# Layer 0's experts: the second expert's gate and up loads stand ahead of the front's loads on SyncE

## The chip, the cores and the metric

The kernel runs on one core of a Trainium2 chip. A core has five engines that run their own instruction streams and meet at semaphores: TensorE (PE, matrix products), VectorE (DVE), ScalarE (ACT), GpSimd (POOL) and SyncE (SP), which here only issues DMA transfers. All transfers of a core share 16 DMA engines. The metric is the device time of one execution in microseconds (us).

## What is computed

Two layers of a transformer trunk over 1024 tokens and 256 context tokens, width 1024, all in float32: a mixer (attention, and in layer 1 a state space scan), then a mixture of 16 experts in which each expert chooses its tokens (128 tokens and 32 context tokens each). The change lies in layer 0's experts:

```python
def expert_choice_ffn(h, w_router, w_gate, w_up, w_down):
    b, n, _ = h.shape
    cap = CAPACITY_FACTOR * n // N_EXPERTS
    aff = jax.nn.softmax(jnp.einsum('bnd,de->bne', h, w_router).astype(jnp.float32), axis=-1)
    gate, idx = lax.top_k(jnp.swapaxes(aff, 1, 2), cap)
    bidx = jnp.arange(b)[:, None, None]
    xg = h[bidx, idx]
    hid = jax.nn.silu(jnp.einsum('becd,edf->becf', xg, w_gate)) * jnp.einsum('becd,edf->becf', xg, w_up)
    out = jnp.einsum('becf,efd->becd', hid, w_down) * gate[..., None].astype(h.dtype)
    return jnp.zeros_like(h).at[bidx, idx].add(out)
...
def trunk_layer(x, ctx, c, c_ctx, common, mixer, ctx_out):
...
    x = x + gt1 * rmsnorm(mix, g_post_mix)
    h = rmsnorm(x, g_pre_ffn) * (1 + sc2) + sh2
    x = x + gt2 * rmsnorm(expert_choice_ffn(h, w_router, w_gate, w_up, w_down), g_post_ffn)
```

Behind it comes layer 1's first part, `front`: the residual sum, its norm and the projections of layer 1.

## The kernel before

`experts` does layer 0's 16 experts one after another. An expert has three weights of 4 MB: gate, up and down, each loaded in two halves of 2 MB (128 partitions x 8 x 512 numbers). There is one buffer for each weight (`wg`, `wu`, `wd`), so a half can be loaded only when the expert before has read it.

On TensorE an expert is `hidden_rows` (eight steps f, each 16 products with gate and 16 with up; steps 0 to 3 read the first half, 4 to 7 the second; `gu_done` counts the steps), `turn_rows` of the next expert's tokens, `down_ctx` (64 products for the context tokens, which need `hid` and `wd`), and seven `multiply` groups that form the down product by a scheme with seven products of half blocks instead of eight. For these VectorE forms sums of blocks of `wd` (`weight_sum`). The first of them, `weight_sum(e, 5)` (L2625), stands in VectorE's stream between the seventh and the eighth `hidden` (L2615), and waits for both halves of `wd`.

SyncE's stream sets the order of the loads. It is written out by hand, and SyncE works it off in that order: a load that waits for a semaphore holds back all behind it. For the first experts it is: gate and up of expert 0, the storing of a third of layer 1's modulation (`store_third`), `wd` of expert 0, a second third, and then

- `following.load`, the loads of layer 1's front (`FrontAhead.load`, L2336 to L2353): 6 loads of 512 KB, 2 of 1 MB and 64 KB (`wk`), 11 of 4 KB that spread a vector over the partitions element by element (`shift`, `gain`, `g`, `cw`), 4 of 4 KB in rows (`alog`, `dtb`)
- `load_gates_up(1)`, gate and up of expert 1 (L2453, L2454), each half behind a wait for `gu_done`: the first half for four steps of expert 0, the second for all eight
- `following.load_columns`, two loads of 2 MB for the front (L2357)
- `load_down(1)`, `wd` of expert 1 (L2461), behind a wait for the last products and sums of expert 0
- a loop over the other experts, each with `load_gates_up` and `load_down`.

What `following` loads goes to buffers of its own and is first read when `front` begins, after the last expert.

Of the kernel before, what the change touches and what calls it, by code (L numbers as in the profile page):

```python
# [153 lines left out]
def columns(ap):  # L154

    return ap.rearrange("(k p) -> p k", p=P)
# [2218 lines left out]
def experts(nc, name, K, listed, normed, mod, g_pre, w_gate, w_up, w_down, moe, following, down, last_third):  # L2375
# [7 lines left out]
    with Stage(nc, name) as st:  # L2383
# [43 lines left out]
        def multiplied(e, p):  # L2427
            return START + e * 7 + (7 + PRODUCTS.index(p) + 1)
# [7 lines left out]
        def sums_at(e, p):  # L2436
            return START + e * 4 + (4 + (5, 7, 6, 4).index(p) + 1)
# [4 lines left out]
        def half_of(weights, e, h):  # L2442
            return weights[bass.ds(e, 1), :, h * BANK:(h + 1) * BANK].rearrange("a (k p) n -> p (a k) n", p=P)

        with nc.Block() as block:

            @block.sync
            def _(sp):
                def load_gates_up(e):

                    for h in range(2):
                        sp.wait_ge(gu_done, START + e * 8 + HALF * (h + 1))
                        sp.dma_start(wg[:, h], half_of(w_gate, e, h)).then_inc(w_in["wg"][h], 16)  # L2453
                        sp.dma_start(wu[:, h], half_of(w_up, e, h)).then_inc(w_in["wu"][h], 16)  # L2454

                def load_down(e):

                    sp.wait_ge(mm_done, multiplied(e - 1, 7))
                    sp.wait_ge(sums_done, sums_at(e - 1, 4))
                    for h in range(2):  # L2460
                        sp.dma_start(wd[:, h], half_of(w_down, e, h)).then_inc(w_in["wd"][h], 16)  # L2461

                for c in range(conds):
                    sp.dma_start(shift[:, c, :], columns(mod[c, 3 * D:4 * D])).then_inc(vec_in, 16)
                    sp.dma_start(gain[:, c, :], columns(mod[c, 4 * D:5 * D])).then_inc(vec_in, 16)
                sp.dma_start(g[:], columns(g_pre)).then_inc(vec_in, 16)
                for n in range(opening.slots, opening.steps):
                    opening.load(sp, n)
                load_gates_up(0)
                opening.store_third(sp, 0)  # L2470
                sp.wait_ge(tp_done, START + 1)
                sp.wait_ge(opening.multiplied, START + opening.steps)
                load_down(0)
                opening.store_third(sp, 1)
                following.load(sp)
                load_gates_up(1)
                following.load_columns(sp)
                load_down(1)
                with sp.Fori(1, E - 1) as e:
                    load_gates_up(e + 1)  # L2480
                    load_down(e + 1)
                for h in range(2):
                    sp.wait_ge(gu_done, START + E * KD + HALF * (h + 1))
                    for n in range(h * HALF, (h + 1) * HALF):
                        closing.load(sp, n)
                st.renew(sp)
                sp.wait_ge(s_done, E * PLACED)
# [1645 lines left out]
```

## Time and profile before

| | us |
|---|---|
| median of 3 runs (3326.73 to 3328.04) | 3327.41 |
| the profiled execution | 3320.73 |
| its span, first to last instruction | 3318.9 |
| TensorE busy in the span | 3094.6 (93%) |
| VectorE, ScalarE, GpSimd busy | 1729.6, 1031.1, 567.1 |

The layer 0 experts run from about 1068 us to 1918 us of the span. The views used below are the timeline of an engine (one line for a run of like instructions: start, duration, engine, source line, tile written and tiles read, and in brackets the idle time before it and what ended it) and the table of stretches, which gives for each stretch the busy time of the engines, TensorE's granted clock as a share of full speed, the mean busy share of the 16 DMA engines and what they moved. On SyncE's timeline a duration is the time until the load is issued; its data land later.

### The profile page before, as it was taken

The page shows a single profiled execution, that of the slowest core. Times are in us where ns is not written, and L with a number is a line of the kernel's source. Part 1 is how long each engine was busy: PE and PEld are TensorE (multiplying, and loading weights), DVE is VectorE, ACT ScalarE, POOL GpSimd, SP SyncE. Part 2 cuts the span into 40 slices and gives each one's busy share as a digit, 9 for nine tenths or more (in the row PEclk, how much of TensorE's full clock was granted, in tenths as well). Part 3 has the DMA queues.
Part 4 walks back from the last instruction along what each step waited for, and adds up shares of the span by engine and source line. Part 5 has one row for each costly group of instructions (what it writes and reads, how often), then busy time and mean ns, then how long its engine had stood idle before and what let it go on. Part 6 is the DMA issues. An engine that isn't in the chain of part 4 may idle for free. (4 is left out here: it accounts for less than half of the span.)

```text
span 3318.9 us, 55367 instructions
## 1 busy us (share of the span) xinstructions
PE 3094.6 (93%) x20487; PEld 2210.7 (67%) x20487; DVE 1729.6 (52%) x3294; ACT 1031.1 (31%) x2319; POOL 567.1 (17%) x685
## 2 busy tenths in 40 slices
PE   6999989989996999999999979999899399999998
PEld 4888855667542888889898855566664255555554
DVE  3312068868646233232333353467785766666666
ACT  4111156756340111111111152245554222222222
POOL 0010224310110111111112130065101101111113
PEclk9999999999996999999999989999899699999999
DMA  6335454043538987778778750122314589999998
GB/s 237 133 111 105 83 190 143 17 110 113 198 146 311 307 308 262 264 261 282 254 262 271 270 192 2 67 72 88 101 34 173 204 303 336 335 333 333 330 330 334
DMA packets 345473, 680.82 MB, mean 205 GB/s; under 512 B 84904, under 2 KB 134056, under 8 KB 339104
## 3 DMA queue, kind: packets, MB, share of 16 engines
q1 hardware_dynamic: 310848, 576.46, 50.2%
q0 software_dynamic: 15920, 47.32, 5.6%
q10 hardware_dynamic: 18560, 55.19, 4.5%
q8 instruction: 81, 1.33, 0.2%
q14 instruction: 64, 0.52, 0.1%
HBM read 594.04 MB, written 91.03 MB: 206 GB/s over the span
## 5 line engine op out<-in xcount | busy, mean ns | idle before, releaser
L2751 PE MATMUL experts_gu_ps<-experts_xT,experts_wg 128*128 128x160 f32 x2048 | 303.2, 301 | 7.7 <-DVEq L2610 5.1
L2751 PE MATMUL experts_gu_ps<-experts_xT,experts_wu 128*128 128x160 f32 x2048 | 299.8, 299 | 0.0
L2751 PEld LDWEIGHTS experts_gu_ps<-experts_xT,experts_wg 128*128 128x128 f32 x2048 | 287.0, 191 | 13.6 <-issue 8.4
L2615 DVE TENSOR_TENSOR experts_hid<-experts_sil,experts_gu_ps 128x160 f32<-128x160 f32 x128 | 41.1, 321 | 489.2 <-ACT experts_sil L2561 489.2
L2751 PEld LDWEIGHTS experts_gu_ps<-experts_xT,experts_wu 128*128 128x128 f32 x2048 | 286.0, 190 | 0.0
L2561 ACT ACTIVATE experts_sil<-experts_gu_ps 128x160 f32<-128x160 f32 x128 | 38.9, 304 | 533.9 <-PE experts_gu_ps L2751 533.9
L3496 PE MATMUL front_pb_ps<-kept_hT,front_ahead_w 128*128 128x512 f32 (+1 forms) x384 | 139.0, 521 | 0.7 <-DVE kept_dt L3562 0.7
L3184 PE MATMUL experts_w_ps<-experts_wd,experts_hT 128*128 128x512 f32 x256 | 130.8, 597 | 8.5 <-issue 7.8
L3184 PE MATMUL experts_v_ps<-experts_wd,experts_hT 128*128 128x512 f32 x256 | 129.6, 592 | 0.0
L563 PE MATMUL proj_x_ps<-first_w,first_shared 128*128 128x256 f32 x480 | 114.7, 382 | 3.1 <-DMA first_w<-in_l_w_in 3.1
L4018 PE MATMUL scan_f_ps<-scan_w,kept_hT 128*128 128x512 f32 x256 | 116.3, 597 | 0.0
L3496 PEld LDWEIGHTS front_pb_ps<-kept_hT,front_ahead_w 128*128 128x128 f32 x384 | 72.3, 190 | 62.7 <-issue 59.4
L2516 POOL DMA_INDIRECT moe<-experts_yc,experts_ixsc x16 | 39.8, 2490 | 432.9 <-ACT experts_yc L2575 432.9
L644 DVE TENSOR_TENSOR proj_ob<-proj_z_ps,proj_kept 128x256 f32<-128x256 f32 x30 | 12.7, 424 | 191.0 <-PE proj_z_ps L563 190.1
L2953 ACT ACTIVATE experts_kept<-experts_x_ps 128x256 f32<-128x256 f32 x96 | 36.9, 384 | 234.6 <-PE experts_x_ps L3176 234.6
L563 PEld LDWEIGHTS proj_x_ps<-first_w,first_shared 128*128 128x128 f32 x480 | 91.5, 191 | 15.8 <-DMA first_w<-in_l_w_in 3.4
L876 ACT ACTIVATE attn_a_e<-attn_a_e,attn_a_nmx 128x1280 f32<-128x1280 f32 (+1 forms) x80 | 96.6, 1209 | 7.5 <-DVE attn_a_e L938 7.5
L2917 POOL DMA_INDIRECT moe<-experts_y,experts_ixs x15 | 24.1, 1609 | 414.3 <-DVE experts_y L3094 414.3
L3184 PEld LDWEIGHTS experts_w_ps<-experts_wd,experts_hT 128*128 128x128 f32 x256 | 47.3, 190 | 65.5 <-issue 64.5
L3184 PEld LDWEIGHTS experts_v_ps<-experts_wd,experts_hT 128*128 128x128 f32 x256 | 48.6, 190 | 61.2 <-issue 61.2
L1038 PE MATMUL attn_a_o_ps<-attn_a_v,attn_a_aT 128*128 128x128 f32 x672 | 83.5, 278 | 3.9 <-ACT attn_a_sq L891 3.9
L938 DVE TENSOR_SCALAR_CACHE_REDUCE attn_a_e<-attn_a_s_ps,attn_a_nmx 128x256 f32<-128x256 f32 (+1 forms) x128 | 72.7, 612 | 27.4 <-PE attn_a_s_ps L1013 27.4
(601 smaller groups left out, 6618.2 us busy)
## 6 DMA issues: line engine op xcount, KB each, us to landing
experts_wg<-in_l_w_gate SPq DMA_DIRECT2D x64, 2048.0 KB, 8.0
experts_wu<-in_l_w_up SPq DMA_DIRECT2D x64, 2048.0 KB, 12.8
down_ahead_wd<-in_l_w_down SPq DMA_DIRECT2D x32, 2048.0 KB, 15.8
experts_wd<-in_l_w_down SPq DMA_DIRECT2D x32, 2048.0 KB, 9.5
down_ahead_wd<-in_l_w_mod SPq DMA_DIRECT2D x16, 1024.0 KB, 9.0
proj<-proj_ob ACTq DMA_DIRECT2D x60, 256.0 KB, 2.3
first_w<-in_l_w_in SPq DMA_DIRECT2D x6, 2048.0 KB, 10.0
attn_a_mod_w<-in_l_w_mod ACTq DMA_DIRECT2D x12, 1024.0 KB, 7.3
```

Of the source, the lines that this page charges most:

```text
L563: mm = nc.tensor.matmul(to[:, left], by[k], at[k], start=(k == 0 and n in (0, 1, 5)), stop=(k == HALF - 1 and n in (3, 5, 6)), skip_group_ ...
L876: nc.scalar.activation(e[:, s, m, 0:w], e[:, s, m, 0:w], ACT.Exp, bias=nmx[:, s, m:m + 1], scale=-1.0, accum_out=sums[:, s, m:m + 1]).then ...
L938: nc.vector.tensor_scalar(e[:, s, m, c:c + w], S[i % 2][m][:, 0:w], -1.0, nmx[:, s, m:m + 1] if j else None, ALU.mult, ALU.min, accum_out= ...
L1038: mm = nc.tensor.matmul(O[:, 0:P], aT[:, kt, :], v[:, h % 2, kt, :], start=(kt * P == keys(t)[0]), stop=(kt == last))
L2516: pool.indirect_dma_start(moe.rearrange("t (j c) -> (t j) c", j=4), bass.IndirectOffsetOnAxis(ap=ixsc[:, 0:1], axis=0), yc[:], None, compu ...
L2561: nc.scalar.activation(sil[:, f % 2, :], GU[f % 2][:, 0, 0:N], ACT.Silu).then_inc(sil_done, 1)
L2615: nc.vector.tensor_tensor(hid[:, f, :], sil[:, f % 2, :], GU[f % 2][:, 1, 0:N], ALU.mult).then_inc(hid_done, 1)
L2751: mm = nc.tensor.matmul(GU[f % 2][:, part, 0:N], w[:, h, k, c * P:(c + 1) * P], xT[:, k, :], start=(k == 0), stop=(k == KD - 1))
L2953: nc.scalar.activation(kept[:, KEPT.index(p), :], bank[:, 0:COLS], ACT.Copy).then_inc(act_out, 1)
L3184: return nc.tensor.matmul(Y[h][:], hT[:, k, :], w[DOWN][:, k, h * BANK:(h + 1) * BANK], start=(k == 0), stop=(k == KD - 1))
L3496: mm = nc.tensor.matmul(pb[n % 4][:, 0:width], w[:, s, k, at:at + P], hT[:, k, first:first + width], start=(k == 0), stop=(k == KD - 1))
L4018: mm = nc.tensor.matmul(F[f % 2][:], kept.hT[:, k, t * P:(t + 1) * P], w[:, int(kind == "q"), k, :], start=(k == 0), stop=(k == KD - 1))
```

## The change

In SyncE's stream the call for expert 1's gate and up loads moves up by one call, over the front's loads. The waits inside the call move with it.

```diff
@@ -2472,8 +2472,8 @@
                 sp.wait_ge(opening.multiplied, START + opening.steps)
                 load_down(0)
                 opening.store_third(sp, 1)
+                load_gates_up(1)
                 following.load(sp)
-                load_gates_up(1)
                 following.load_columns(sp)
                 load_down(1)
                 with sp.Fori(1, E - 1) as e:
```

No other engine's stream differs. On SyncE, where the front's loads begin (`signal103` is `gu_done`; `signal81` and `signal82` count the sums and the stores of the modulation):

```order
 L2461 DMA down_ahead_wd<-in_l_w_down 128x8x512
 L266 DMA mod<-experts_shared 2x512 [waits signal81] x4
-L2338 DMA front_ahead_gate<-mod 128x1024 [waits signal82]
-L2338 DMA front_ahead_gate<-mod 128x1024
+L2453 DMA experts_wg<-in_l_w_gate 128x8x512 [waits signal103,signal82]
+L2454 DMA experts_wu<-in_l_w_up 128x8x512
+L2453 DMA experts_wg<-in_l_w_gate 128x8x512 [waits signal103]
+L2454 DMA experts_wu<-in_l_w_up 128x8x512
+L2338 DMA front_ahead_gate<-mod 128x1024 x2
 L2339 DMA front_ahead_gpost<-in_l_g_post_ffn 128x1024
 L2341 DMA front_ahead_xt<-res 128x1024 x3
```

The four gate and up loads now follow the modulation's store, and the front's first load stands behind the second wait for `gu_done`.

On SyncE, where the front's small loads end and expert 1's down weights follow (`signal106` and `signal109` are the counts that `load_down` waits for):

```order
 L2352 DMA front_ahead_cw<-in_l_conv_w 128x8x1 x5
 L2353 DMA front_ahead_cw<-in_l_conv_b 128x8x1
-L2453 DMA experts_wg<-in_l_w_gate 128x8x512 [waits signal103]
-L2454 DMA experts_wu<-in_l_w_up 128x8x512
-L2453 DMA experts_wg<-in_l_w_gate 128x8x512 [waits signal103]
-L2454 DMA experts_wu<-in_l_w_up 128x8x512
 L2357 DMA front_ahead_w<-in_l_w_in 128x8x512 x2
 L2461 DMA down_ahead_wd<-in_l_w_down 128x8x512 [waits signal109,signal106]
```

The front's small loads now run straight into its column loads and the down weights, which have the same loads ahead of them as before, in another order.

## Rows read from the trace of the kernel before

**Rows 1.** The page: its span, and TensorE's busy time, share and instructions.

```profile
span 3318.9 us, 55367 instructions
PE 3094.6 (93%) x20487; PEld 2210.7 (67%) x20487; DVE 1729.6 (52%) x3294; ACT 1031.1 (31%) x2319; POOL 567.1 (17%) x685
```

**Rows 2.** Timeline of TensorE, experts 0 to 3: start us, us, what, [idle before].

```profile
1068.02 3.91 PE L2751 MATMUL experts_gu_ps<-experts_xT,experts_wg 128*128 128x160 f32 x16 [5.13 <-DVEq L2610]
...
1084.81 2.34 PE L2751 MATMUL experts_gu_ps<-experts_xT,experts_wu 128*128 128x160 f32 x16
...
1102.20 2.34 PE L2751 MATMUL experts_gu_ps<-experts_xT,experts_wu 128*128 128x160 f32 x16
...
1119.95 1.90 PE L2714 MATMUL experts_y_ps<-experts_shared,experts_hid 128*64 128x256 f32 x16
1124.38 3.42 PE L2751 MATMUL experts_gu_ps<-experts_xT,experts_wg 128*128 128x160 f32 x16 [2.54 <-DMA experts_wu<-in_l_w_up]
1127.59 3.07 PE L2751 MATMUL experts_gu_ps<-experts_xT,experts_wu 128*128 128x160 f32 x16
...
1163.86 3.66 PE L2725 MATMUL experts_yc_ps<-down_ahead_wd,experts_hid 128*32 128x256 f32 x64 [1.28 <-DVE experts_hid L2615]
...
1179.69 2.44 PE L2751 MATMUL experts_gu_ps<-experts_xT,experts_wg 128*128 128x160 f32 x16
...
1195.00 2.34 PE L2751 MATMUL experts_gu_ps<-experts_xT,experts_wu 128*128 128x160 f32 x16
...
1231.97 2.44 PE L2751 MATMUL experts_gu_ps<-experts_xT,experts_wg 128*128 128x160 f32 x16
```

**Rows 3.** Timeline of VectorE around the second expert's first weight sum.

```profile
1157.20 0.32 DVE L2615 TENSOR_TENSOR experts_hid<-experts_sil,experts_gu_ps 128x160 f32<-128x160 f32 x1 [4.03 <-ACT experts_sil L2561]
1161.28 2.29 DVE L2625 TENSOR_TENSOR experts_shared<-down_ahead_wd 128x2048 f32<-128x2048 f32 x1 [3.76 <-DMA down_ahead_wd<-in_l_w_down]
1163.49 0.31 DVE L2615 TENSOR_TENSOR experts_hid<-experts_sil,experts_gu_ps 128x160 f32<-128x160 f32 x1
```

**Rows 4.** Timeline of SyncE's queue: start of issue us, us until issued.

```profile
1085.13 0.82 SPq L2338 DMA_DIRECT2D front_ahead_gate<-mod  x2
...
1108.32 0.58 SPq L2453 DMA_DIRECT2D experts_wg<-in_l_w_gate  x1
...
1120.65 13.07 SPq L2357 DMA_DIRECT2D front_ahead_w<-in_l_w_in  x2
1133.83 12.46 SPq L2461 DMA_DIRECT2D down_ahead_wd<-in_l_w_down  x2
...
1197.52 0.38 SPq L2453 DMA_DIRECT2D experts_wg<-in_l_w_gate  x1
...
1214.89 0.37 SPq L2453 DMA_DIRECT2D experts_wg<-in_l_w_gate  x1
```

**Rows 5.** Stretches: us, engines' busy us, granted clock, DMA share, GB/s.

```profile
1197.60:1850.00 652.40, 652.40 (x5611) 576.40 (x5611) 214.66 (x330) 94.98 (x227) 109.42 (x157) 1.00 0.78 266
...
1085.00:1086.00 1.00, 1.00 (x9) 1.00 (x9) 0.00 (x0) 0.00 (x0) 0.00 (x0) 1.00 0.06 25
...
1085.00:1110.20 25.20, 25.20 (x230) 23.20 (x231) 7.91 (x17) 3.49 (x10) 0.00 (x0) 1.00 0.83 177
1110.20:1161.20 51.00, 48.46 (x367) 44.30 (x364) 10.42 (x14) 5.33 (x13) 8.99 (x13) 0.97 1.05 372
...
1209.00:1211.00 2.00, 2.00 (x17) 2.00 (x16) 0.17 (x1) 0.30 (x1) 0.00 (x0) 1.00 0.60 220
1211.00:1213.00 2.00, 2.00 (x17) 2.00 (x16) 1.96 (x2) 0.00 (x0) 0.00 (x0) 1.00 0.00 0
1213.00:1215.00 2.00, 2.00 (x17) 2.00 (x16) 0.48 (x1) 0.16 (x1) 0.00 (x0) 1.00 0.00 0
1215.00:1216.00 1.00, 1.00 (x14) 0.83 (x12) 0.79 (x3) 0.15 (x1) 0.00 (x0) 1.00 0.11 6
1216.00:1217.00 1.00, 1.00 (x20) 0.65 (x22) 0.97 (x3) 0.75 (x3) 0.00 (x0) 1.00 0.87 137
```

## The prediction

> **What bounds the kernel now.** I began with the page. TensorE is busy for 93% of the span of 3318.9 us [rows 1], so the kernel is ahead wherever TensorE does not wait, and what a change of loads can move is the few places where it does. The stretches of time tell where these are: from 1197.6 us, in the third expert's gate products, to 1850 us TensorE is busy for 652.40 of 652.40 us [rows 5]. From there one expert takes 52.28 us (1179.69 to 1231.97, [rows 2]), and whatever shift the third expert starts with goes through to the end. So only the first two experts matter, and the timeline of TensorE shows two waits there [rows 2]:
>
> First, after the first expert's down products (last start 1119.95, 1.90 us) TensorE stands still until 1124.38, 2.54 us, released by the up weights `wu` of the second expert. After the stop its first two groups of 16 take 3.42 and 3.07 us, where the third expert's first takes 2.44 and the others 2.34: 1.71 us more. This is what the change goes for: 2.5 + 1.7, some 4.3 us.
>
> Second, at 1163.86 it starts the second expert's context products 1.28 us late, released by VectorE's last product for `hid`. The timeline of VectorE tells why that was late [rows 3]: VectorE is in order, and ahead of the last `hidden` stands `weight_sum(e, 5)` (L2625), which reads the down weights `wd`. It waited 3.76 us for them and began at 1161.28. So the landing of `wd` of the second expert sets the time at which TensorE goes on at 1163.86, and **TensorE arrives there early already**. Had the first wait not been there, the second would be 1.28 + 4.3 = 5.6 us long, and the third expert would begin when it does now. The question is then not how early the gate and up weights come but when `wd` lands.
>
> When it lands is a matter of the queue. The timeline of SyncE [rows 4] has the front's loads from 1085.13, the second expert's gate and up loads from 1108.32, the front's two column loads from 1120.65, `wd` from 1133.83. The stretches [rows 5] show the 16 DMA engines at a share of 0.83 from 1085 to 1110.2 and at 1.05 from 1110.2 to 1161.2: packed without a hole until `wd` is there. That landing moves by what is added to the queue ahead of it, bytes or holes.
>
> **The change, part by part.** No instruction and no byte is added or taken away; on SyncE four loads of 2 MB stand ahead of 23 loads of the front instead of behind them, and all 27 still stand ahead of `wd`. What changes is when the queue has something to do.
>
> (a) The first half of gate and up waits for TensorE to have read that half (`gu_done`). The front's first load now starts at 1085.13; the fourth pair of groups of the first expert ends at 1084.81 + 2.34 = 1087.15 [rows 2]. With the 0.15 us that such a load needs after its release (1197.34 to 1197.52 in the third expert, [rows 4]), the queue gets its first work at 1087.3, 2.2 us later than now.
>
> (b) The second half waits for all eight, 1102.20 + 2.34 = 1104.54 [rows 2], so it is issued at 1104.7. Behind this wait the front's 23 loads are queued, and nobody else feeds the queue. Before the change this wait cost nothing, because the loads stood so late that both halves were free. How long the queue stands empty is shown by a later expert, where the same two halves are issued 17.37 us apart (1197.52 and 1214.89, [rows 4]); here it is 17.4. There the share is 0.60 in 1209 to 1211, 0.00 until 1215, 0.11 in 1215 to 1216, 0.87 in the next us [rows 5]. Data end near 1210.2 and begin again near 1215.9: **a hole of 5.7 us**. In a later expert there is slack for it; here there is none.
>
> (c) The second expert's gate and up weights are then there by about 1100 and 1118 (issue plus 12.7 us as in the third expert: 1197.52 to 1210.2), TensorE wants them at 1121.8 and 17 us later. The first wait goes.
>
> (d) The front's loads are wanted after the last expert, beyond 1850 us; late by tens of us they cost nothing.
>
> (e) `wd` lands 2.2 + 5.7 = 7.9 us later, since what is ahead of it is the same. VectorE begins L2625 at 1161.28 + 7.9 = 1169.2 instead of 1161.28, and TensorE its context products at 1171.8 instead of 1163.86. It is free for them at 1162.58 - 4.3 = 1158.3, so it waits 13.5 us. Bounds of the 7.9: below, the front's stretch may pack better when a backlog stands before it. Its share of 0.83 over 25.2 us leaves 4.3 us unused, 0.9 of them at its start (0.06 in the first us, [rows 5]); so up to 3.4 us could come back, and 4.5 us be left. I take none of it: the stretch now has rows first and then many small loads of 4-byte elements, which SyncE must issue one after another in either order. Above, the first half moves its 4.19 MB in 12.7 less some 0.9 to begin, 11.8 us, where the 372 GB/s of the packed stretch make 11.3: 0.5 us more, and as much again for what GpSimd's transfers may do.
>
> (f) TensorE's clock. After the stop of 2.54 us the granted share fell and 1.71 us were lost; at 1068.02, after a stop of 5.13 us, the first group took 3.91 instead of 2.44, 1.5 us lost [rows 2]. Now a stop of 13.5 us stands ahead of the context products. Between 1.5 and 3.4 us (twice the 1.7); I take 1.9, near to the two rows, a little above since the stop is longer than either. The old loss of 1.7 no longer counts on the path, as it lay ahead of a wait that it only shortened.
>
> (g) After that: the third expert's first gate and up half stands right behind `wd`, 4.19 MB, 11.3 us by the same rate, there at some 1181; TensorE wants it at 1179.69 + 9.8 = 1189.5. Second half and next `wd` have more room. Nothing late comes after.
>
> **Sum:** 7.9 + 1.9 = 9.8 us slower. The profiled execution took 3320.73 us, 6.7 less than the median of the runs (3327.41), with a span of 3318.9; by it the new one would be 3330.5, its span 3328.7. I put the same difference on the median: 3337.2 us.
>
> **A rule that speaks for a smaller number.** Of the 25.2 us up to 1110.2 the queue's engines leave 17% unused [rows 5]. The Trainium skill, DMA: Bandwidth & Descriptors, section Bandwidth, gives 0.68 us for a 4 KB transfer (issued from GpSimd, where these come from SyncE). By it the front's 11 small column loads would be 7.5 us of the queue, and at the trace's rate the 4.2 MB of rows and key columns 11.3: 18.8 us for a stretch that now takes some 24. If a backlog hid all the rest, `wd` would land 2.5 us late and the sum be 4.4 us, an estimate from that page; it is the far end of R1 below. The trace's share leaves less room than that, and no row shows these loads behind a backlog.
>
> **Rivals.**
> *R1, the front's stretch packs.* As bounded in (e): `wd` lands 4.5 us late, the clock costs 1.5 to 1.9, the sum is 6.0 to 6.4, 3333.6 us. For it: 0.83 is not 1.05. Against: in the stretch SyncE issues without end from 1085.13 to 1108.32, 23.2 us, so that issuing is itself near the limit. It lies just inside 0.2% (6.7 us, 3334.1 us), which is about what a measurement of this kernel can tell from no change.
> *R2, faster: the gate and up wait was the real one.* If `wd` lands so early that VectorE finds it when it asks (1157.52 - 4.3 = 1153.2), TensorE gains 2.5 + 1.7 + 1.3 = 5.6 us: 3321.8 us. This needs `wd` to land 8 us earlier than now, by later loads overtaking the front's. For it only that the loads differ in kind; against it that the first wait ended with `wu`, which was behind the front's loads, and the share of 1.05. Every `wd` between costs or gains its own shift, and at an unmoved landing the change is worth 0 (3327.4).
> *R3, worse than forecast.* The clock takes 3.4 and the hole is longer by the gathers' traffic and the slower first half, 2 to 4 us: some 3341 to 3343. It decides from the point at which the third expert's weights land behind TensorE, 8 us later than in (g).
>
> **Chances.** Forecast (7.9 with its clock cost, 3334.5 to 3340) 0.66; R1 0.14; R2 0.07; an unmoved landing 0.04; R3 0.09. Faster by over 0.2%: half of R2 and little else reach 3320.8, and R2 stands 0.17% away, so 0.04. Slower by over 0.2%: the forecast, R3 and a third of R1, 0.79. Within: 0.17. The range leaves out R2 and the unmoved landing and the far end of R3: 3332.8 to 3341.
>
> **What would show it.** In the changed kernel: the first gate load of the second expert at 1087.3 and the third at 1104.7 on SyncE, a share of nearly 0 in between from 1100 to 1105.7; no wait of TensorE at 1121.8 and none for `wu`; the front's loads issued from 1106 to about 1140; VectorE's wait for `wd` at L2625 of some 16 us where 3.76 stand; TensorE's wait ahead of the context products of 13.5 us, and a granted clock below 1 behind it; the third expert's first gate product at 1189.5; everything later as before. I am wrong if `wd` lands before 1165, which would be the front's loads packing, or if TensorE does not wait there at all.

## The result, and the profile after

The change makes the kernel slower: a median of 3334.43 us over 15 runs against 3325.4 us over 15 runs of the kernel before, ratio 1.0022 with a 95% interval of 1.0016 to 1.0029. On 3325.4 us that is 7.3 us, 5.3 to 9.6; the plain difference of the two medians is 9.0 us, that of the two means 8.1. The forecast was 9.8 us: the direction and the mechanism held, the size was too large, and its sum lies just outside the interval. Of the 2.8 us between the forecast time, 3337.2, and the median, 2.0 are the start of the sum, 3327.41 from three runs, where fifteen give 3325.4. The two profiled executions (3330.26 and 3320.73 us) are single numbers in a spread of 6.5 us over runs of one kernel, so the traces are read below from a mark inside them.

TensorE of the changed kernel, with the columns of [rows 2]:

```profile
1069.36 4.55 PE L2751 MATMUL experts_gu_ps<-experts_xT,experts_wg 128*128 128x160 f32 x16 [5.14 <-DVEq L2610]
...
1075.92 2.34 PE L2751 MATMUL experts_gu_ps<-experts_xT,experts_wg 128*128 128x160 f32 x16
...
1123.74 2.44 PE L2751 MATMUL experts_gu_ps<-experts_xT,experts_wg 128*128 128x160 f32 x16
...
1171.94 5.68 PE L2725 MATMUL experts_yc_ps<-down_ahead_wd,experts_hid 128*32 128x256 f32 x64 [11.67 <-DVE experts_hid L2615]
...
1189.79 2.44 PE L2751 MATMUL experts_gu_ps<-experts_xT,experts_wg 128*128 128x160 f32 x16
...
1242.07 2.44 PE L2751 MATMUL experts_gu_ps<-experts_xT,experts_wg 128*128 128x160 f32 x16
```

The span is 3328.5 us. The wait for the up weights ahead of expert 1 is gone. In its place TensorE stands 11.67 us ahead of the context products, and these then take 5.68 us instead of 3.66. Expert 0 already began 1.3 us later in this execution and its first group took 0.6 more, which has nothing to do with the change, whose first moved load is issued only at 1089.23. So I count from expert 0's second step (1073.94 in the trace of before, 1075.92 here) to the first gate group of the fourth expert (1231.97 and 1242.07): 158.03 us before, 166.15 after, 8.1 more. Below this stretch is called **the interval**.

VectorE and SyncE of the changed kernel, which answer to [rows 3, 4]:

```profile
1169.36 2.29 DVE L2625 TENSOR_TENSOR experts_shared<-down_ahead_wd 128x2048 f32<-128x2048 f32 x1 [14.15 <-DMA down_ahead_wd<-in_l_w_down]
```

```profile
1089.23 0.39 SPq L2453 DMA_DIRECT2D experts_wg<-in_l_w_gate  x1
...
1106.54 0.37 SPq L2453 DMA_DIRECT2D experts_wg<-in_l_w_gate  x1
...
1107.87 3.99 SPq L2338 DMA_DIRECT2D front_ahead_gate<-mod  x2
...
1145.94 8.44 SPq L2461 DMA_DIRECT2D down_ahead_wd<-in_l_w_down  x2
```

VectorE waits 14.15 us for `wd` where it waited 3.76. SyncE issues the two halves of gate and up 17.3 us apart (1089.23 and 1106.54), and between them nothing. The stretches of the changed kernel show what the 16 DMA engines did meanwhile (columns as in [rows 5]; the share is the last but one):

```profile
1101.00:1103.00 2.00, 2.00 (x17) 2.00 (x16) 0.33 (x2) 0.30 (x1) 0.00 (x0) 1.00 0.39 143
1103.00:1105.00 2.00, 2.00 (x17) 2.00 (x17) 2.00 (x1) 0.00 (x0) 0.00 (x0) 1.00 0.00 0
1105.00:1107.00 2.00, 2.00 (x19) 2.00 (x17) 0.32 (x2) 0.30 (x1) 0.00 (x0) 1.00 0.00 0
1107.00:1109.00 2.00, 2.00 (x32) 1.39 (x34) 1.93 (x6) 0.98 (x3) 0.00 (x0) 1.00 0.65 124
```

By the shares, data end near 1101.8 and begin again near 1107.7, a hole of 5.9 us (5.7 were forecast).

### The profile page after: what moved, and what is told of

Same layout as the page of the kernel before. It is cut to its first block and busy times, and to the rows that moved or that the text cites. A ratio compares the mean times of both kernels' runs of the same rounds, so it can differ in the third digit from the quotient of the medians.

```text
span 3328.5 us, 55368 instructions
## 1 busy us (share of the span) xinstructions
PE 3095.2 (93%) x20487; PEld 2211.0 (66%) x20487; DVE 1728.7 (52%) x3294; ACT 1030.8 (31%) x2319; POOL 566.7 (17%) x685
```

## The experiments

My theory: the landing of expert 1's `wd` sets when the third expert begins; what comes ahead of it in the queue, bytes or holes, decides, and the wait for the up weights is worth nothing by itself. The main rival is that the early weights or their order against the front's loads cost by themselves. All edits are to the few lines in SyncE's stream, unless the text says otherwise. A ratio is the time against that of the kernel before, with its 95% interval. "Landing" below is the landing of `wd`'s second half, issue plus time to landing, counted from expert 0's second step.

### A second look at both kernels

Nothing is edited here.

> The kernel before once more, for a second trace. Question: how far the times of expert 1 vary from run to run when nothing is changed. In the experiment with wd ahead of the column loads TensorE's wait for the up weights was 1.1 us instead of 2.5 and the front's first load stood 1.7 us earlier against expert 0's steps. If that is only the run, these waits are again between 1 and 3 us here and the wait of VectorE for wd between 2 and 4.

> The changed kernel once more, for a second trace. Theory: its first gate load hangs on expert 0's fourth step and not on the modulation's store, so its times counted from expert 0's steps repeat within some 0.3 us: L2625 at 93.4 us after the second step, context products 5.2 to 5.7 us.

The kernel before, second trace:

```profile
1076.92 2.34 PE L2751 MATMUL experts_gu_ps<-experts_xT,experts_wg 128*128 128x160 f32 x16
...
1126.65 2.44 PE L2751 MATMUL experts_gu_ps<-experts_xT,experts_wg 128*128 128x160 f32 x16 [1.83 <-DMA experts_wu<-in_l_w_up]
...
1166.21 5.35 PE L2725 MATMUL experts_yc_ps<-down_ahead_wd,experts_hid 128*32 128x256 f32 x64 [3.04 <-DVE experts_hid L2615]
...
1236.01 2.44 PE L2751 MATMUL experts_gu_ps<-experts_xT,experts_wg 128*128 128x160 f32 x16
```

This trace alone shows that the first wait was covered. It is 1.83 us instead of 2.54 and the groups behind it lose nothing to the clock, so TensorE is 2.4 us earlier at the second wait; and there it waits 3.04 us instead of 1.28. VectorE's wait for `wd` was 5.52 us, beyond the 2 to 4 written down, and `wd` landed at 86.4 against 87.0. The clock's loss of 1.7 us now stands behind the second wait (5.35 against 3.66), where it counts: the interval is 159.09, against 158.03. The kernel before thus varies by itself, and its mean of two is 158.6 us.

The changed kernel repeated: L2625 at 93.2 us after the second step (93.4), the wait 11.45 (11.67), context products 5.66 (5.68), the interval 165.92 (166.15). Mean against mean the change costs 7.5 us (6.8 and 8.1 by single pairs), in agreement with the runs. `wd` lands at 86.7 before and 93.1 after: 6.4 us later.

### Only the first half ahead of the front's loads

Against the changed kernel:

```diff
-                load_gates_up(1)
+                load_gates_up(1, [0])
                 following.load(sp)
+                load_gates_up(1, [1])
                 following.load_columns(sp)
                 load_down(1)
```

(`load_gates_up` got a list of halves as an argument.)

> The changed kernel, but only the first half of expert 1's gate and up stands ahead of the front's loads; the second half, with its wait for all eight steps, stands behind them. Ahead of wd are the same loads, the queue starts as late as in the change (2.1 us), but has no hole. Theory (wd's landing sets the end, and holes in the queue move it): VectorE begins L2625 2.1 us later than in the kernel before, counted from expert 0's steps, TensorE waits 7 to 8 us ahead of the context products, the clock takes 1.5 to 2: 3.6 to 4 us slower than before. Rival A (the front's loads take longer once weights stand ahead of them, the hole is beside the point): as the change, 8 us slower. Rival B (the lost time is the early weights themselves, any such order costs the same): 8 us too.

```profile
1077.73 2.34 PE L2752 MATMUL experts_gu_ps<-experts_xT,experts_wg 128*128 128x160 f32 x16
...
1125.56 2.44 PE L2752 MATMUL experts_gu_ps<-experts_xT,experts_wg 128*128 128x160 f32 x16
...
1167.82 5.31 PE L2726 MATMUL experts_yc_ps<-down_ahead_wd,experts_hid 128*32 128x256 f32 x64 [5.73 <-DVE experts_hid L2616]
...
1237.58 2.44 PE L2752 MATMUL experts_gu_ps<-experts_xT,experts_wg 128*128 128x160 f32 x16
```

Ratio 1.0009 (1.0000 to 1.0018), interval 159.85 us. Rivals A and B, who had this as slow as the change, are out: it is 6.2 us shorter. The wait for the up weights is gone here too, and the context products begin 90.1 us after the second step, where they begin at 89.9 and 89.3 in the kernel before. **Taking the first wait away is worth nothing as long as `wd` does not land earlier.** `wd` landed at 87.2 us, 5.9 us before the change's (93.1). Both kernels start the queue at the same point, 13.3 us after the second step; they differ in the hole, 5.9 us long, and in the place of the second half against the front's loads. That the hole costs what it lasts fits both numbers; no run has the one without the other.

But I had expected the landing 2.1 us later than in the kernel before, a wait of TensorE of 7 to 8 us and a loss of 3.6 to 4. The first gate load stands at 13.3 us here and the front's first load at 11.2 and 10.1 there, so the queue starts 2.1 and 3.2 us later. The landing was 0.2 and 0.8 later, the wait 5.73, the interval 1.3 us longer than the mean of before. Something ahead of `wd` took 1.9 to 2.4 us less.

### The term that was too large

Two theories for it: the front's rows move faster when weights stand ahead of them, or GpSimd's gathers and scatters, 5 to 6 us of the DMA engines, are hidden in the front's small loads once these run later. The share of 0.83 in [rows 5] had suggested that the small loads leave room. To separate them, the 17 front's loads behind the six of 512 KB go behind `wd`, once in the kernel before and once in the changed one. The first, with a new method `load_small` for the second part of `FrontAhead.load`:

```diff
                 following.load(sp)
                 load_gates_up(1)
                 following.load_columns(sp)
                 load_down(1)
+                following.load_small(sp)
```

and the second with `load_gates_up(1)` ahead of `following.load(sp)`.

> The kernel before, but of the front's loads ahead of gate and up only the six of 512 KB stay; the 17 others (key columns, 4-byte columns, rates) stand behind wd of expert 1. One look for the queue: the 17 take some 15 us of it in the kernel before, so wd, now 87 us after expert 0's second step, lands 14 to 15 us sooner. TensorE waits for nothing in expert 1; the third expert's weights may then be late by what moved ahead of them, as nothing left the queue ahead of these.

> The same in the changed kernel. The question is the term that came out too large: wd lands 6.3 us later in the change, 7.9 were forecast. Theory H (GpSimd's gathers and scatters, 5 to 6 us of the DMA engines, ran in the packed stretch before and now run inside the front's small loads, which leave part of the engines free): with the small loads gone from ahead of wd nothing hides GpSimd's traffic any more, so wd lands only 12 to 13 us sooner than in the change. Rival (the front's rows alone got faster behind a backlog, by 1.5 us, and the small loads cost the same in both places): 14 to 15 us sooner, as in the kernel before.

`wd` landed at 72.9 us in the first, 13.8 us sooner than in the kernel before (86.7), and at 79.3 in the second, 13.8 us sooner than in the changed one (93.1). In the first SyncE has to wait 2.8 us for expert 0's products before it may issue `wd`, but the queue stays full meanwhile (a share of 1.03 or more in every us from 1118 to 1129). The small loads cost the queue the same in both places, and the difference of 6.4 us stays when they are gone. Theory H wanted 12 to 13 in the second, so this speaks against it, by 0.8 us in one trace. The rival's 14 to 15 is missed by 0.2 as well, but its claim, that both are alike, holds. For it speaks the rate of the six row loads, which one can read where next to nothing else runs beside them. In the kernel before they are the first in the queue, right behind the modulation's store:

```profile
1086.20:1094.20 8.00, 8.00 (x61) 8.00 (x61) 0.64 (x2) 0.61 (x2) 0.00 (x0) 1.00 0.99 320
...
1087.00:1091.00 4.00, 4.00 (x32) 4.00 (x31) 0.32 (x1) 0.30 (x1) 0.00 (x0) 1.00 0.99 264
1091.00:1095.00 4.00, 4.00 (x32) 4.00 (x30) 0.32 (x1) 0.30 (x1) 0.00 (x0) 1.00 1.02 398
```

Behind the first half of the weights, in the experiment above, and behind both halves, in the changed kernel:

```profile
1103.50:1110.00 6.50, 6.50 (x60) 6.21 (x62) 3.81 (x6) 0.77 (x3) 0.00 (x0) 1.00 1.03 410
```

```profile
1122.00:1127.00 5.00, 5.00 (x42) 4.18 (x39) 0.97 (x2) 1.76 (x2) 3.11 (x2) 1.00 1.03 416
```

The same 3.1 MB go at 320 GB/s on the mean (307 in the second trace) where they are the first in the queue, and at 410 to 416 behind weights: by these rates 10.0 us on the mean of the two traces against 7.7, at a share near 1 in either. Nearly the whole loss lies in their first five us, with 264 GB/s from 1087 on; from 1091 they run at 398. Weights at the head of the queue start slowly too, but not for as long. In the experiment above, their first two us and the nine behind them:

```profile
1092.00:1094.00 2.00, 2.00 (x17) 2.00 (x16) 0.00 (x0) 0.00 (x0) 0.00 (x0) 1.00 0.87 222
1094.00:1103.00 9.00, 9.00 (x69) 9.00 (x68) 0.64 (x2) 0.61 (x2) 0.00 (x0) 1.00 1.04 393
```

That takes 0.9 us back from the 2.3, and leaves about 1.4: the size of the forecast's error of 1.5, and most of the 1.9 to 2.4 us between these traces, the rest of which is open. Why the rows start more slowly than the weights was not tried: that they have just been stored, or how they are read.

The first of the two kernels also shows TensorE without any wait in expert 1, interval 152.40; one run took 3321.86 us. In the second the third expert's weights came late instead, a wait of 4.11 us, interval 157.94; its one run took 3325.50.

### `wd` ahead of the column loads, in the kernel before

```diff
                 following.load(sp)
                 load_gates_up(1)
-                following.load_columns(sp)
                 load_down(1)
+                following.load_columns(sp)
```

> The kernel before, but wd of expert 1 stands ahead of the front's two column loads; the front's other loads still stand ahead of gate and up. Theory: the wait for the up weights stays at 2.5 us, wd lands some 11 us (4.2 MB) earlier, VectorE's wait of 3.76 us and TensorE's of 1.28 go: 1.3 us faster. Rival (wd is not what VectorE waits for, or the queue does not land loads in their order): no difference, the waits stay.

Ratio 0.9989 (0.9979 to 0.9998), 3.7 us faster. VectorE's and TensorE's waits for `wd` are gone as expected, which the rival excluded. The interval is 153.59, 5.0 less than the mean of before and not 1.3. TensorE waited 1.1 us for the up weights in this trace and its clock stayed at full level:

```profile
1127.95 2.44 PE L2751 MATMUL experts_gu_ps<-experts_xT,experts_wg 128*128 128x160 f32 x16 [1.14 <-DMA experts_wu<-in_l_w_up]
```

My 1.3 took the waits of one trace for fixed. An early `wd` removes the second wait and its clock. Then nothing covers the first wait any more, and what is left of the loss is what this wait happens to be in a run: 1.1 us here, by luck, where 2.54 and 1.83 were seen before.

### `wd` ahead of the column loads, in the changed kernel

The same edit in the changed kernel: gate and up, front, `wd`, columns.

> The changed kernel, but wd of expert 1 stands ahead of the front's two column loads. Theory: wd lands 10.9 us earlier than in the change, VectorE begins L2625 at 1156.5 on the clock of the kernel before, waits 3.3 us, TensorE waits 0.8 us, the clock keeps its level; 4.7 us faster than the kernel before and 13 faster than the change. Rival (the change loses by its hole or its clock whatever wd does): still 4 to 8 us slower than before.

Ratio 1.0003 (0.9993 to 1.0012), no difference from the kernel before, where I expected 4.7 us faster. Up to the context products all went about as written: VectorE waits 2.59 us (3.3 expected), TensorE not at all (0.8), and it begins them 84.5 us after the second step, 5.1 us earlier than the mean of before. Then

```profile
1182.49 3.87 PE L2751 MATMUL experts_gu_ps<-experts_xT,experts_wg 128*128 128x160 f32 x16 [3.71 <-DMA experts_wu<-in_l_w_up]
```

the third expert waits 3.71 us for its own up weights, and its first group loses 1.4 to the clock. The column loads had moved from ahead of `wd` to ahead of these, and the hole of 5.9 us stands ahead of both. I had followed the queue only to the wait that I wanted away. The rival, 4 to 8 us slower whatever `wd` does, is out as well: moving `wd` alone gave back the change's whole loss (interval 157.78, against 166.0 in the change and 158.6 before).

### No hole, and `wd` ahead of the column loads

Against the changed kernel:

```diff
-                load_gates_up(1)
+                load_gates_up(1, [0])
                 following.load(sp)
-                following.load_columns(sp)
+                load_gates_up(1, [1])
                 load_down(1)
+                following.load_columns(sp)
```

> First half of gate and up, the front's small loads, second half, wd, the front's column loads. No hole and wd early. Theory: neither VectorE nor TensorE waits in the first two experts; the third expert begins 5.6 us earlier than in the kernel before: 5.6 us faster. It fails if the second half lands after TensorE wants it, 17.4 us into expert 1, by my sum 1 us ahead of it: then 1 to 3 us of that are lost again. Rival (the front's loads take longer behind a backlog): the second half is late by that, 4 us or more.

Ratio 0.9984 (0.9975 to 0.9993): 5.3 us faster than the kernel before, median 3320.82 us. The interval is 152.40:

```profile
1126.30 2.44 PE L2752 MATMUL experts_gu_ps<-experts_xT,experts_wg 128*128 128x160 f32 x16
...
1162.75 3.66 PE L2726 MATMUL experts_yc_ps<-down_ahead_wd,experts_hid 128*32 128x256 f32 x64
...
1178.58 2.44 PE L2752 MATMUL experts_gu_ps<-experts_xT,experts_wg 128*128 128x160 f32 x16
```

From expert 0's second step to the fourth expert no row of TensorE has an idle time; an expert takes 52.28 us. This is the version to keep, and the expected 5.6 us lie within the 2.3 to 8.3 of the ratio.

### The clock

In this pair TensorE's first two experts are written out ahead of its loop. The one has products of the identity with itself while TensorE waits for `wd` in expert 1, the other is its control.

```diff
+                    if warm:
+                        pe.wait_ge(yc_out, START + e)
+                        keep_warm(nc, K, YC, warm)
                     pe.wait_ge(hid_done, START + e * KD + KD)
                     down_ctx(e)
```

> The same with experts 0 and 1 written out and no extra products, the control of the one above: as the changed kernel, 8 us slower than before, context products of expert 1 near 5.7 us. If writing the loop out costs or gains by itself, it shows here.

> The changed kernel, with experts 0 and 1 written out ahead of TensorE's loop, and 80 products of the identity with itself (some 10 us of TensorE's work, into the bank of the context products, which is overwritten) while it waits for wd in expert 1. Theory: wd lands when it did, TensorE begins the context products at the same time, but with the clock at full level, so that they take 3.66 us and not 5.68: 2 us faster than the changed kernel, 6 slower than the kernel before. Rival (the 5.68 us are not the clock but the products waiting for something of their own): no gain over the kernel with the same loop written out and no extra products.

> The 80 extra products took TensorE 18.13 us in the trace, not some 10, and overran the wait for wd. Here there are 46 (10.4 us at that rate), which end before wd lands. Theory: context products of expert 1 take 3.66 us and not 5.3 to 5.7, so the third expert begins 1.6 to 2 us sooner than in the same kernel without them: 2 us faster than it, some 6 slower than the kernel before.

The control is 1.0024 (1.0015 to 1.0033), as the change, with an interval of 166.73. Its L2625 stands 94.4 us after the second step, and in the two kernels with extra products at 95.4 and 94.3, where the changed kernel has 93.4 and 93.2. What delays `wd` by 1 to 2 us once the two experts are written out is not known; so these kernels are compared with their control alone. The 80 products were mis-sized, as one float32 product shows as two rows of the trace: 18.13 us, beyond the landing, 1.0038 (1.0024 to 1.0052), interval 170.46. That run still shows context products of 3.66 us. With 46, and a wait of 2.07 us left behind them:

```profile
1161.62 10.54 PE L151 MATMUL experts_yc_ps<-ident 128*128 128x128 f32 x92
...
1174.22 3.66 PE L2725 MATMUL experts_yc_ps<-down_ahead_wd,experts_hid 128*32 128x256 f32 x64 [2.07 <-DVE experts_hid L2615]
```

The stretch of the context products shows the granted clock as the third number from the end, in this kernel and in the control:

```profile
1174.20:1177.80 3.60, 3.58 (x64) 1.98 (x64) 3.53 (x10) 0.00 (x0) 0.00 (x0) 1.00 1.05 388
```

```profile
1177.90:1183.10 5.20, 5.20 (x66) 2.42 (x66) 3.52 (x10) 0.00 (x0) 0.00 (x0) 0.68 1.04 386
```

3.66 us at full clock, where the control took 5.28 at 0.68; the interval is 165.00, 1.7 us less than the control's. So the clock is the cause of those 1.6 us (2.0 in the change), not a wait of the products. The runs don't show it: 1.0030 (1.0018 to 1.0042) against 1.0024 (1.0015 to 1.0033), both intervals being wider than the effect. By its time alone the experiment is inconclusive, and the size rests on the trace.

## Why the prediction was right or wrong

- **The first wait is covered, and `wd` sets the third expert's start.** Right. The kernel with the first half alone ahead has no first wait and begins its context products when the kernel before does.
- **The queue begins 2.2 us later** (a). Right by the trace that it was read from: the first gate load stands 13.3 us after the second step, the front's first load at 11.2 there, 2.1 less; in the second trace of before it is at 10.1, 3.2 less.
- **A hole of 5.7 us** (b). Right: 5.9 in the trace, and 5.9 as the difference in landing from the kernel without it.
- **"What is ahead of it is the same", so `wd` lands 7.9 us late** (e). The bytes are the same, their time is not. It landed 6.4 us late. The lower bound of 4.5 allowed for a saving, but I took none of it, and I looked for it in the small loads with their share of 0.83, where the pair with these loads moved shows none. It is mostly in the rows, which I had left at what they took at the queue's head, and whose share of about 1 hid that they ran at 320 GB/s and not at 410. This is the step that failed: a saving put at nothing, worth 1.5 us against the forecast's 7.9, and 2.2 against the terms as they measured (2.7 for the start on the mean of both traces, and 5.9). The size is small beside what a landing does by itself: 0.6 us between the two traces of before, and up to 2.2 with the kernels of the section on the clock.
- **The clock, 1.9 us** (f). 2.0 in both traces of the change, 1.6 in the control. Wrong was to say that the kernel before pays nothing for it on the path: in the second of its two traces it pays 1.7 at the same place. The term of the difference is then between 0.3 and 2.0, where I counted 1.9.
- **TensorE's wait of 13.5 us.** 11.67 and 11.45. TensorE was free when forecast (84.3 us after the second step); L2625 came at 93.4, where the sum had 95.2 counted from the one trace. It is the miss of (e) once more.
- **Nothing is late behind it** (g). Right for the change: the third expert begins without a wait. The experiment with `wd` ahead of the columns shows that this was near: with other loads in that place it waited 3.71 us.
- **R1**, the front's stretch packs: a part of it happened, at another place than it names. The far end of it, a landing only 2.5 us late, is not borne out: the 17 loads cost 13.8 us of the queue with a backlog as without. The Trainium skill, DMA: Bandwidth & Descriptors, section Bandwidth, has 0.68 us for a 4 KB transfer from GpSimd, and the estimate from it was 7.5 us for 11 of these 17, which spread their 4 KB element by element; no run times the 11 by themselves. R2 is out: every trace of the change has `wd` late. R3 did not happen.
- **The sum.** 6.4 for the landing and 0.3 to 2.0 for the clock are 6.7 to 8.4 us; 7.5 by the traces, 7.3 by the runs. 9.8 came from two terms that were too large: the landing by 1.5 us, the clock by 0 or 1.7, as the kernel before happens to run.

## What to carry to other kernels

A wait is worth its time only if nothing behind it waits longer for something that the edit does not bring sooner; look for the next wait on the same path and ask what sets it. On an in-order queue a load moved forward takes its semaphore wait with it, and the queue runs dry if that wait outlasts what was issued ahead of it (here 5.9 us of a wait of 15.2): move only the loads whose buffers are already free, and leave the others behind work that can fill the time. When loads change places, follow the queue to every later load that shares it, not only to the one that was late.

## What the runs showed of the hardware

Six row loads of 512 KB, as the first in an empty queue and behind a store, ran at 264 GB/s over four of their first five us and then at 398, and at 410 to 416 behind weights, at a busy share of the DMA engines of 0.99 to 1.03 in all of these stretches: the share does not tell the rate.

Stops of TensorE of 1.14, 1.28, 1.83 and 2.07 us left the granted clock at 1.00, the level of 2.4 GHz, for what came next. Stops of 2.54, 3.04, 3.71, 4.11 and 5.73 us were each followed by 1.4 to 1.7 us lost at the lower level, 1.2 GHz (granted 0.50 in 1172 to 1176 of the changed kernel, for one). The loss did not grow with the stop: 2.0 us after 11.45 and 11.67, 1.6 after 12.66, and 1.5 to 2.3 after the stop of 5.1 to 5.2 us ahead of expert 0 that every trace has.
